# Six borders between stages of a fused transformer kernel: one step for the norm sums, two engines for the high parts, the next weights' parts moved, filler matmuls in the gaps

## What is computed

```python
x = x + 0.5 * m2 * rmsnorm(swiglu(modulate(rmsnorm(x, g), m0, m1)))      # ffn1
x = x + m5 * rmsnorm(mixer(modulate(rmsnorm(x, g), m3, m4)))             # mix1
x = x + 0.5 * m8 * rmsnorm(swiglu(modulate(rmsnorm(x, g), m6, m7)))      # ffn2
for l in range(2):
    x = x + mixer2(rmsnorm(x, attn_norm_w[l]))                           # mix2_0, mix2_1
    x = x + peer_ffn(rmsnorm(x, ffn_norm_w[l]))                          # peer_0, peer_1
```

## Time and profile before

| | us |
|---|---|
| median of three executions | 2501.21 (2501.13 to 2502.32) |
| the profiled execution | 2501.28 |
| its span, first to last instruction | 2499.5 |

### The profile page before, as it was taken

The page is one execution under the profiler, slowest core; times in us unless marked ns, Lnnn a source line. Parts: engine busy times, 40 slices in busy tenths (PEclk is TensorE's granted clock), DMA queues, the critical chain, the costliest instruction groups (busy, mean ns, idle before and its releaser), DMA issues.

```text
span 2499.5 us, 39122 instructions
## 1 busy us (share of the span) xinstructions
PE 2422.9 (97%) x15670; PEld 2110.7 (84%) x15670; DVE 1794.2 (72%) x3443; ACT 1258.9 (50%) x1805; POOL 346.1 (14%) x297
## 2 busy tenths in 40 slices
PE   7998998998999999999999999999999999999999
PEld 7987878988888888888888887888888888888887
DVE  8887666656545778888887555744778888988555
ACT  3544655445455565555444545454565555444444
POOL 3022101003333610000000001440730000000000
PEclk9999999999899999999999999899999999999999
DMA  9797334554324554444545555224455444454554
GB/s 388 261 348 252 120 135 169 214 199 159 111 94 171 184 186 177 173 170 157 184 170 207 191 197 191 104 102 154 169 187 184 170 169 172 171 180 170 214 188 152
DMA packets 73029, 455.77 MB, mean 182 GB/s; under 512 B 9099, under 2 KB 15371, under 8 KB 20754
## 3 DMA queue, kind: packets, MB, share of 16 engines
q1 hardware_dynamic: 72162, 452.21, 50.9%
q0 software_dynamic: 688, 1.06, 0.3%
HBM read 449.17 MB, written 4.06 MB: 181 GB/s over the span
## 4 chain that ended last, share of the span: by engine, by line
PE 85%; DVE 8%; ACT 3%; POOL 1%; issue 1%; DMA 0%; SPq 0%; DVEq 0%; POOLq 0%; ACTq 0%
PE ps L378 19%; PE ps L351 16%; PE ps L352 16%; PE ps L353 16%; PE ps L380 8%; PE ps L2522 2%; PE ps L397 1%; DVE wlo L333 1%; ACT whi L314 1%; PE ps L377 1%; DVE raw L344 1%; DVE XB L1207 1%; ACT xn L474 1%; PE ps L2502 1%; PE ps L1136 1%
## 5 line engine op out<-in xcount | busy, mean ns | idle before, releaser
L314 ACT ACTIVATE whi<-raw 128x1024 fp32r<-128x1024 f32 x765 | 809.5, 1060 | 1045.6 <-PE ps L353 642.0
L333 DVE TENSOR_TENSOR wlo<-raw,whi 128x1024 fp32r<-128x1024 f32 x670 | 819.3, 1226 | 513.3 <-ACT whi L314 513.0
L378 PE MATMUL ps<-HT,whi 128*128 128x512 f32 x2048 | 718.7, 399 | 0.0
L380 PE MATMUL ps<-HT,wlo 128*128 128x256 f32 x1792 | 502.1, 280 | 0.0
L378 PEld LDWEIGHTS ps<-HT,whi 128*128 128x128 f32 x2048 | 372.3, 188 | 68.9
L351 PE MATMUL ps<-whi,CT 128*128 128x512 f32 x1024 | 404.0, 395 | 1.2 <-DVE wlo L333 0.9
L352 PE MATMUL ps<-wlo,CT 128*128 128x512 f32 x1024 | 398.7, 389 | 0.0
L353 PE MATMUL ps<-whi,CT 128*128 128x512 f32 x1024 | 398.6, 389 | 0.0
L380 PEld LDWEIGHTS ps<-HT,wlo 128*128 128x128 f32 x1792 | 338.5, 189 | 8.6
L351 PE MATMUL ps<-HT,whi 128*128 128x256 f32 x968 | 279.6, 289 | 3.2 <-DVE wlo L333 1.2
L352 PE MATMUL ps<-HT,whi 128*128 128x256 f32 x968 | 275.8, 285 | 0.0
(11 more groups left out here) (393 smaller groups left out, 3312.6 us busy)
## 6 DMA issues: line engine op xcount, KB each, us to landing
raw<-in_down SPq DMA_DIRECT2D x128, 1024.0 KB, 4.8
raw<-in_up SPq DMA_DIRECT2D x128, 1024.0 KB, 4.8
raw<-in_w_in SPq DMA_DIRECT2D x41, 1024.0 KB, 4.9
raw<-in_ffn_gu SPq DMA_DIRECT2D x36, 1024.0 KB, 4.9
raw<-in_w_ada SPq DMA_DIRECT2D x28, 1024.0 KB, 6.2
raw<-in_ffn_d SPq DMA_DIRECT2D x22, 1024.0 KB, 5.6
raw<-in_w_out SPq DMA_DIRECT2D x12, 1024.0 KB, 4.8
raw<-in_w_ada SPq DMA_DIRECT2D x16, 512.0 KB, 13.4
```

Source lines behind the costliest of these rows:

```text
L314: e.activation(self.whi[:, i % NSPLIT, :], self.raw_of(i), ACT.Copy, bias=0.0, scale=1.0).then_inc(*k.inc("w_hi", ("hi", i)))
L333: e.tensor_tensor(self.wlo[:, n, :], self.raw_of(i), self.whi[:, n, :].bitcast(F32), ALU.subtract).then_inc(*k.inc("w_lo_pool" if pool els ...
L378: t = e.matmul(out.rearrange("p (a t) -> p a t", a=2), hi[:, s], self.HT[:, c, :, :], start=c == 0, stop=c == 7)
L380: t = e.matmul(out[:, 0:T], lo[:, s], self.HH[:, c, :], start=False, stop=False)
```

## The change

- `sums_pool`: the three POOL steps become two. One `tensor_scalar` takes the first sum, adds the second (a per-partition scalar) and the epsilon; it waits for both sums. Then the power.
- `ON_POOL` gains the slots 66, 99, 165, 201, 465 and 501. POOL makes the new stage's first `wlo` behind the power of half 1; DVE no longer makes it.
- At a border ACT makes `whi` of slot `end` between half 0's sums and its scaling (peer to mix2, mix2 to peer), or behind the result's squares of half 0 (ffn, mix1), and `whi` of `end + 1` behind the sums of half 1. It no longer scales half 1.
- DVE scales half 1 alone, both pieces (`norm_scale_dve(..., 1, (0, 1))`); half 0's piece comes one multiplication earlier in ffn and mix1.
- `norm_apply_act` / `norm_apply_dve`: without a shift (mix2, peer) ACT writes `HH` for c = 0, 1, 4, 5 and DVE for c = 2, 3, 6, 7. Then DVE makes `wlo` of slot `end + 1`, and only then the eight `HL`. With a shift (mix1, ffn2) ACT keeps all eight `HH`, and DVE makes that `wlo` behind the four first `f`.
- `warm`: PE multiplies the identity by itself (128x128, float32) into a part of bank 0 that is overwritten later: ahead of half 0's transposes 4 times (ffn) or 8 times (mix1), between the halves 20 times (ffn, mix1) or 10 times (the others).

```diff
-ON_POOL = set(range(1, 14, 2)) | {82, 84}
+ON_POOL = set(range(1, 14, 2)) | {66, 82, 84, 99, 165, 201, 465, 501}
...
     def sums_pool(self, e, what, st):
         k = self.k
-        for w in k.late(("sq", *what, 0)):
-            e.wait_ge(*w)
-        e.tensor_scalar(st[:, 0:1], st[:, 0:1], D * EPS, None, ALU.add).then_inc(*k.inc("pool_norm", ("eps", *what)))
-        for w in k.late(("eps", *what), ("sq", *what, 1)):
-            e.wait_ge(*w)
-        e.tensor_tensor(st[:, 2:3], st[:, 0:1], st[:, 1:2], ALU.add).then_inc(*k.inc("pool_norm", ("sum", *what)))
+        for w in k.late(("sq", *what, 0), ("sq", *what, 1)):
+            e.wait_ge(*w)
+        e.tensor_scalar(st[:, 2:3], st[:, 0:1], st[:, 1:2], D * EPS, ALU.add, ALU.add).then_inc(*k.inc("pool_norm", ("sum", *what)))
...
+    def warm(self, e, count):
+        for w in self.k.late("ident in", *self.free[0]):
+            e.wait_ge(*w)
+        for _ in range(count):
+            e.matmul(self.ps[:, 0, 128:256], self.ident[:, :], self.ident[:, :], start=True, stop=True)
...
     def norm_apply_act(self, e, n, gain, shift, need):
-        for c in range(8):
+        for c in range(8) if shift is not None else (0, 1, 4, 5):
...
-    def norm_apply_dve(self, e, n, gain, shift, f, need):
+    def norm_apply_dve(self, e, n, gain, shift, f, need, end):
         k = self.k
+        if shift is None:
+            for c in (2, 3, 6, 7):
+                b = c // 2
+                for w in k.late(self.turned(n, b), *need):
+                    e.wait_ge(*w)
+                e.tensor_scalar(self.HH[:, c, :], self.ps[:, b, 256 * (c % 2):256 * (c % 2) + 256], gain[:, c:c + 1], None,
+                                ALU.mult).then_inc(*k.inc("dve_hh", ("hh", n, c)))
+            self.lo(e, end + 1)
...
+            if shift is not None and b == 1:
+                self.lo(e, end + 1)
...
     def close_act(self, e, n, end, after):
         self.norm_sums_act(e, n, 0, after)
+        self.hi(e, end)
         self.norm_scale_act(e, n, 0)
-        self.hi(e, end)
         self.norm_sums_act(e, n, 1, after)
         self.hi(e, end + 1)
-        self.norm_scale_act(e, n, 1)

     def close_dve(self, e, n, end, ready, after):
         self.add_y(e, n, 0, lambda h: ready(0, h), after)
         self.norm_scale_dve(e, n, 0)
         self.add_y(e, n, 1, lambda h: ready(1, h), after)
-        self.lo(e, end)
-        self.norm_scale_dve(e, n, 1)
-        self.lo(e, end + 1)
+        self.norm_scale_dve(e, n, 1, (0, 1))

     def close_pool(self, e, n, end):
-        self.sums_pool(e, (n, 0), self.st[:, 0, 0, :])
-        self.lo(e, end, True)
-        self.sums_pool(e, (n, 1), self.st[:, 1, 0, :])
+        for tt in range(2):
+            self.sums_pool(e, (n, tt), self.st[:, tt, 0, :])
         self.lo(e, end + 1, True)
```

More of the change, by code:

```diff
@@ L498, in rstd_pool, with norm_scale_dve @@
         e.tensor_tensor(out, out, self.mhalf[:, 0:width], ALU.pow).then_inc(*k.inc("pool_norm", ("rstd", *what)))
-    def norm_scale_dve(self, e, n, tt):
+    def norm_scale_dve(self, e, n, tt, halves=(0,)):
         k = self.k
-        for w in k.late(("rs", n, tt)):
-            e.wait_ge(*w)
-        e.tensor_scalar(self.xn[n][tt][:, 0:512], self.x[:, tt, 0:512], self.st[:, tt, 0, 2:3], None,
-                        ALU.mult).then_inc(*k.inc("dve_norm", ("xn", n, tt, 0)))
+        for h in halves:
+            w0 = slice(512 * h, 512 * h + 512)
+            for w in k.late(("rs", n, tt)):
+                e.wait_ge(*w)
+            e.tensor_scalar(self.xn[n][tt][:, w0], self.x[:, tt, w0], self.st[:, tt, 0, 2:3], None,
+                            ALU.mult).then_inc(*k.inc("dve_norm", ("xn", n, tt, h)))
     def norm_scale_act(self, e, n, tt):
@@ L551, in norm_apply_dve @@
                 src, g = self.ps[:, b, 256 * (c % 2):256 * (c % 2) + 256], gain[:, c:c + 1]
-                for w in k.late(self.turned(n, b), ("hh", n, 2 * b + 1), *need):
+                for w in k.late(self.turned(n, b), ("hh", n, 2 * b + 1), ("hh", n, c), *need):
                     e.wait_ge(*w)
@@ L642, in residual_mul @@
         for h in range(2):
+            if h and tt:
+                self.norm_scale_dve(e, n, 0)
             for w in k.late(("sq", "res", n, tt, h), (tag, "gb", 1)):
@@ L1004, in ffn_pe @@
         for tt in range(2):
+            self.warm(e, (4, 20)[tt])
             self.norm_turn(e, n + 1, tt)
@@ L1040, in ffn_act @@
             if tt:
+                self.norm_scale_act(e, n + 1, 0)
+            else:
                 self.hi(e, end)
-                self.norm_scale_act(e, n + 1, 0)
             self.norm_sums_act(e, n + 1, tt, done)
-            if tt:
-                self.hi(e, end + 1)
-                self.norm_scale_act(e, n + 1, 1)
+        self.hi(e, end + 1)
     def ffn_dve(self, e, t):
@@ L1052, in ffn_dve @@
         else:
-            self.norm_apply_dve(e, n, self.md[:, 0:8], self.md[:, 8:16], t.f, [("gain", 6)])
+            self.norm_apply_dve(e, n, self.md[:, 0:8], self.md[:, 8:16], t.f, [("gain", 6)], t.slot)
         for c in range(t.first, F_CH):
@@ L1480, in outputs @@
                 self.residual_act(e, n + 1, tt, [t.Z[:, tt, h, :] for h in range(2)], lambda h: (tag, "ty", tt, h), done)
-                if tt:
+                if tt == 0:
                     self.hi(e, end)
+                else:
                     self.norm_scale_act(e, n + 1, 0)
@@ L1532, in mixer1_dve @@
             e.wait_ge(*w)
-        self.norm_apply_dve(e, n, self.md[:, 0:8], self.md[:, 8:16], t.f, [("gain", 3)])
+        self.norm_apply_dve(e, n, self.md[:, 0:8], self.md[:, 8:16], t.f, [("gain", 3)], t.slot)
         for w in k.late("w_idx in"):
@@ L1654, in outputs @@
                 self.residual_mul(e, n + 1, tt, [t.Z[:, tt, h, :] for h in range(2)], t.GB, tag, t.Z2[:, tt, :, :])
[L1655 to L1656 removed]
                 self.residual_add(e, n + 1, tt, t.Z2[:, tt, :, :])
                 if tt:
[L1659 to L1661 removed]
+                    self.norm_scale_dve(e, n + 1, 1, (0, 1))
         def proj(r):
@@ L2187, in mixer2_dve @@
         k, PS, n, tag, l = self.k, self.ps, t.n, t.tag, t.l
-        self.norm_apply_dve(e, n, self.norms[:, l, :], None, None, ["norms"])
+        self.norm_apply_dve(e, n, self.norms[:, l, :], None, None, ["norms"], t.slot)
         for w in k.late(("c2", l)):
@@ L2653, in peer_dve @@
         k, PS, n, tag = self.k, self.ps, t.n, t.tag
-        self.norm_apply_dve(e, n, self.norms[:, 2 + t.l, :], None, None, ["norms"])
+        self.norm_apply_dve(e, n, self.norms[:, 2 + t.l, :], None, None, ["norms"], t.slot)
         def best(what, step, src, val, ind, tmp, rows, need):
```

15 lines of the change are left out of this document (4 added, 11 removed).

## The result

The changed kernel took 2522.03 us at the median of four executions (2519.16 to 2527.45), beside 2501.17 for the kernel before on the same chip; the ratio is 1.0085, 95% interval 1.0065 to 1.0105. It is slower by some 21 us. In two of its executions the mean granted clock was 0.993 of full speed and the time 2519 us, in the other two it was 0.989 and 0.988 and the time 2524.68 and 2527.45. Its profiled execution took 2519.39 us with a span of 2516.8, that is +17.3 in the span, 2.6 us under its own median.

The account below looks back on a forecast made before the run. PE, busy nearly throughout, was taken as the bound, its border waits set by DVE and POOL chains. Border shifts of 16.05 us plus 1.0 for half clock, +17.0 on 2501.28, gave 2518.3 us; range 2500 to 2524.

Parts of the forecast that it names:

- The sums, 0.35 us per border: At each border, one POOL step fewer, with DVE's `wlo` gone beside it, ends the power 0.35 us earlier.
- POOL's `wlo` wins the race: At each border POOL's `wlo` starts first and holds DVE's scaling; half 1's transposes start 1.78 us later; chance 0.60.
- Rival B: At the borders DVE's scaling gets in before POOL's `wlo`: +5.2 us, 2506.5 (2503 to 2509); chance 0.25.
- Rival C: Faster: clock and PE's own work set each border's end, 7.89 us from transposes to third slot; 2492.6; chance 0.13.
- The scaling's second piece costs nothing: Half 1's scaling by DVE alone: second piece ends 0.45 us behind the first, hidden by four transposes; no cost.
- HH, `wlo`, HL in series: DVE's longer chain delays the third slot: T + 10.84 us in mix2, `wlo` at T + 8.05 in peers (T: half 1's transposes).
- mix1, 2.9 us: Border into mix1: HH 1.39 us later, added `wlo` 1.2, meeting POOL's HL 0.3; +2.9 us, all seen by PE.
- Fillers: At the borders ten take 1.1 us, twenty 2.2; they delay nothing but don't secure the full clock.
- Shifts carried to the end in full: Behind each border PE's shift moves every engine's next work, so all border shifts, 16.05 us together, reach the end.
- the clock term: Half clock on PE's way behind idle gaps at borders and before mix2 third slots: 1.0 us added (0 to 6).

Follow-up runs that it names:

- the kernel with the parts kept: Kernel before plus one-step sums, fitted fillers, HH six ACT/two DVE, mix1 `wlo` before the table wait, mix2 third-slot `wlo` on DVE: 2489.99 us, ratio 0.9963.

## Why the prediction came out as it did

- **The sums, 0.35 us per border.** Right in the changed kernel (0.32 from read to power), since DVE is idle beside it; alone it is 0.2, since the step then takes 0.45.
- **POOL's `wlo` wins the race.** Right, at all six borders. DVE's first piece took 2.56 us, and half 1's transposes came 1.73 to 2.11 us later against 1.78 forecast. With POOL made to wait, they came 2.07 earlier at the last three borders. The rule of the Trainium skill that I had set beside the earlier trace rows ("SBUF — State Buffer", "SBUF: two separate sides") gave the right sign. Rival B, DVE first, gave 2506.5 and didn't take place; forced by a wait, it gave 2513.2, higher mainly because mix1 cost 6.9 us there, against 0.8 by that rival (2.9 less 2.13). Rival C, each border at PE's own pace, describes not this change but the kernel with the parts kept: 7.06 and 7.20 us from the transposes to the third slot in the mix2 stages against its 7.89, though 9.00 and 8.81 in mix1 and ffn2, and 2490.0 against its 2492.6.
- **The scaling's second piece costs nothing.** Right: eight transposes follow without a pause, in 1.09 us.
- **HH, `wlo`, HL in series.** Right. T to the third slot was 10.62 and 11.05 us in the mix2 stages (599.49 to 610.11, 1559.71 to 1570.76) against 10.84 reckoned, and 7.90 in both peers against 8.05. Alone on the kernel before, this part cost 10.6 us in the medians, with 4.5 of it at mix1.
- **mix1, 2.9 us: the step that failed.** It measured 8.38. I had counted the added `wlo` in DVE's chain, but not who waits for that `wlo`: SP's load, the index table behind it in SP's queue, DVE's cast, the third slot's `wlo` behind the cast. The kernel with `wlo` ahead of the cast showed 1.84 there. Two more things that the term didn't hold: the table's transfer took some 2.4 us longer (cause open), and the half clock behind PE's 6.81 us of waiting made the stage behind 2.1 us longer.
- **Fillers.** The term was mis-sized: 0.11 us each was read from the transposes, of which each is one instruction, while such a float32 matmul is two; a filler is 0.23 us, ten 2.3, twenty 4.6. From this I had concluded that an idle of 3.1 to 3.5 us stays behind them and that they don't secure the clock. It was 1.0 to 2.1 us and all six groups of transposes ran at full clock. The conclusion on time, near nothing, held by the medians (2522.2 without them), in part for another reason: PE waited for a `wlo` behind them anyhow, 6.81, 3.10 and 3.10 us at three borders and 0.4 at the other three. Border by border it holds less well: 3.9 us at five of them, covered by 2.0 at mix1 that came from a faster transfer. As for the Trainium skill's price of slow clock ("TensorE: Matmul & The Clock Gate", "HAM oscillation"), some 30 us less at half clock would by its half be 15 us won; the runs with and without fillers show 0 (medians) to 3 us (profiled executions) here, and 4 us, the sums and the luck of the mix2 stages included, where they are fitted.
- **Shifts carried to the end in full.** Wrong for the mix2 stages, which gave back 6.6 us. A shift is harmless only where nothing else has its own time; POOL's `wlo` and DVE's convolution meet or miss each other by some tenths of a us.

In the span the misses are +5.5 and +2.1 around mix1, -6.6 in the mix2 stages, +0.8 ahead of the first border and -1.0 for the clock term, which nothing here shows by itself; they nearly cancel, so that the forecast of 2518.3 looks better than its parts (2519.39 in the profiled execution, 2522.03 in the median). Five borders' terms and the race were right by themselves; that the total is right is partly luck.

## What to carry to other kernels

Before a step is moved, write down who waits for it and what is queued behind each of these waiters, the DMA queue first: the dearest miss here was four links long. Giving POOL work that begins when DVE is released by the same event cost DVE the whole of POOL's instruction here, for the kinds of operation named below; look for such pairs in the timeline by operations of DVE that take 2 us more than their kind, and move those off POOL one at a time. Size fillers from their own rows in a trace, and expect their clock to pay where PE has its own work behind them (1.35 us at each peer border here), not where it waits.

## What the runs showed of the hardware that I had not expected

- A float32 matmul of 128 columns stands in the trace as two instructions: 20 of them as 40 in 4.63 us. A transpose of the same shape is one: eight in 1.09 us.
- Not every operation of DVE is held beside POOL's `wlo`. Held were `tensor_scalar` from SBUF (the scaling, 2.56 instead of 0.49) and operations with two inputs from SBUF (the convolution steps, `wlo`). In the kernel before all 64 MAX8 over 128x128 took 0.27 to 0.29 us, and all 128 additions of a PSUM bank to `AST` (L2832) 0.68 to 0.69 us; one of these began at 877.21, 0.14 us behind a `wlo` of POOL.
- A single POOL instruction, off the path by itself, was worth 3.6 us of a stage (half of the 7.2 us in the medians): 2.1 us held from DVE, PE's wait behind it, and half clock for 6.8 us behind that wait.
- Starting first isn't quite the rule of who holds whom. In the kernel before a convolution step of DVE began at 629.37, 0.03 us ahead of POOL's `wlo`, and took 2.66 us where its neighbours take 0.48. At 1587.97 it was the same. A step into `MIX` with two inputs from SBUF at 710.35, 0.05 us ahead of a `wlo` of POOL, took its usual 0.41. POOL's times in a profile are rough, so these hundredths may be its error:

```profile
629.37 2.66 DVE L1207 SCALAR_TENSOR_TENSOR XB<-XR,c,XB 128x254 f32<-128x254 f32 x1
629.40 2.35 POOL L333 TENSOR_TENSOR wlo<-raw,whi 128x1024 fp32r<-128x1024 f32 x1
```

- Such meetings make a stage's length jump. Among the kernels that leave the assignment of the mix2 slots behind the borders as it was, the two mix2 stages, from the third slot to the last 512-wide matmul, lasted 161.4 and 162.0 us before, 159.2 and 157.7 in the changed kernel, and 162.6 in the second one where POOL waits for the scaling.
